# Gathered-expert work planned by stage instead of at one even spacing, in a two-block transformer kernel

## What is computed

```python
# first block: window attention + spatial gating + pooling, gated and merged;
#              memory attention; dense MLP (1024 -> 4096 -> 1024)
# second block: MLA attention (8 heads) and forgetting attention (8 heads), o @ w_o, and then
h2 = _modulate(x, norm2_g, shift2, scale2)
x = x + gate2 * _peer(h2, w_pq, sub_keys, peer_u, peer_v)

def _peer(h, w_pq, sub_keys, peer_u, peer_v):
    qp = (h @ w_pq)...                      # 8 heads x 2 halves of 128
    s1, i1 = lax.top_k(sc[..., 0, :], 16); s2, i2 = lax.top_k(sc[..., 1, :], 16)
    top_s, top_c = lax.top_k(all 16 x 16 sums, 16)
    expert = e1 * 128 + e2; gate = softmax(top_s)       # 16 experts a head, of 16384
    a = h . peer_u[expert]                  # one dot product of 1024 for each expert
    y = sum(gate * gelu(a) * peer_v[expert])
```

## Time and profile before

| | |
|---|---|
| median of 3 runs | 2723.76 us |
| the profiled execution | 2719.11 us, its span 2717.3 us |
| busy in the span | PE 2066.2 us, DVE 1366.1, POOL 1158.2, ACT 457.1 |
| first half's dense part | 0 to 918 us |
| second half's dense part, with the first half's experts | 918 to 1972.8 us |
| the second half's experts alone | 1972.8 to 2717.3 us |

### The profile page before, as it was taken

One profiled execution on the slowest core, in us unless ns is written; L12 is line 12 of the kernel. 1 busy time (PEld: TensorE's weight loads), 2 busy tenths in 40 slices (PEclk: granted clock), 3 DMA queues, 4 the chain that ended last, 5 costly groups with the idle time before them and its releaser, 6 DMA issues.

```text
span 2717.3 us, 27166 instructions
## 1 busy us (share of the span) xinstructions
PE 2066.2 (76%) x9658; PEld 1441.0 (53%) x9658; DVE 1366.1 (50%) x3057; ACT 457.1 (17%) x1123; POOL 1158.2 (43%) x1090
## 2 busy tenths in 40 slices
PE   7899989999989979997999998888923332323334
PEld 5788778887466767875777773454800000000001
DVE  1302136302424986557654466753657575766641
ACT  2311131001442222112210012332100000000000
POOL 2000002000001456544545553454477777777775
PEclk9899989998969989997899988889965556655557
DMA  6244329642415979997999998789799999999998
GB/s 226 69 152 149 132 90 376 214 155 85 136 34 175 390 301 359 394 396 269 341 392 386 381 346 313 281 307 340 264 335 382 352 368 354 379 359 364 367 407 349
DMA packets 214728, 779.19 MB, mean 287 GB/s; under 512 B 23891, under 2 KB 26515, under 8 KB 213571
## 3 DMA queue, kind: packets, MB, share of 16 engines
q0 software_dynamic: 155136, 564.97, 55.0%
q1 hardware_dynamic: 57272, 207.44, 21.5%
q10 hardware_dynamic: 2187, 5.05, 0.5%
HBM read 770.78 MB, written 6.58 MB: 286 GB/s over the span
## 4 chain that ended last, share of the span: by engine, by line
PE 59%; POOL 18%; issue 9%; DVE 8%; DMA 4%; ACT 2%; ACTq 0%; DVEq 0%; POOLq 0%
PE bank L563 43%; POOL main L499 18%; PE bank L732 5%; DMA main<-in_peer_v,idx_v 3%; PE bank L631 3%; PE bank L668 2%; PE bank L686 2%; DVE main L1479 1%; DMA main<-in_peer_u,idx 1%; PE bank L677 1%; PE bank L640 1%; PE bank L980 1%; ACT main L1012 1%; PE bank L694 0%; DVE main L1401 0%
## 5 line engine op out<-in xcount | busy, mean ns | idle before, releaser
L563 PE MATMUL bank<-main,ring 128*128 128x256 f32 x4864 | 1076.8, 383 | 10.3 <-DVE main L1636 4.0
L563 PEld LDWEIGHTS bank<-main,ring 128*128 128x128 f32 x4864 | 928.8, 192 | 167.5 <-issue 28.4
L499 POOL DMA_INDIRECT main<-in_peer_v,idx_v x512 | 550.5, 1075 | 458.5 <-PE bank L732 315.7
L732 PE MATMUL bank<-main,w_wide 128*32 128x512 f32 x2048 | 370.3, 860 | 440.3 <-DMA main<-in_peer_v,idx_v 416.1
L499 POOL DMA_INDIRECT main<-in_peer_u,idx x512 | 570.5, 1114 | 311.7 <-issue 148.5
L1479 DVE CUSTOM_DVE_ANT_0 main<-main 128x1024 f32<-128x1024 f32 x256 | 313.8, 1226 | 245.0 <-DMA main<-in_peer_u,idx 241.4
L732 PEld LDWEIGHTS bank<-main,w_wide 128*32 128x32 f32 x2048 | 73.4, 138 | 670.2 <-issue 669.2
L1479 DVE CUSTOM_DVE_ANT_0 main<-main,h_a 128x1024 f32<-128x1024 f32 x256 | 313.8, 1226 | 203.6 <-DMA main<-in_peer_u,idx 198.0
L1012 ACT ACTIVATE main<-bank 128x256 f32<-128x256 f32 (+4 forms) x346 | 145.6, 439 | 775.6 <-PE bank L563 747.9
L563 PE MATMUL bank<-ring,main 128*128 128x512 f32 (+3 forms) x624 | 239.2, 544 | 9.5 <-ACT main L1012 8.8
L492 POOL DMA_DIRECT2D main<-in_w_ada x48 | 25.3, 533 | 451.8 <-DVE main L1656 451.8
(11 more groups left out here) (219 smaller groups left out, 1368.6 us busy)
## 6 DMA issues: line engine op xcount, KB each, us to landing
ring<-in_w_stream SPq DMA_DIRECT2D x370, 512.0 KB, 5.7
main<-in_w_ada POOLq DMA_DIRECT2D x48, 512.0 KB, 7.3
main<-in_peer_u,idx POOLq DMA_INDIRECT x512, 6.6
main<-in_peer_v,idx_v POOLq DMA_INDIRECT x512, 6.5
main<-in_sub_keys SPq DMA_DIRECT2D x2, 1024.0 KB, 9.3
main<-rows_d SPq DMA_DIRECT2D x1, 1536.0 KB, 10.2
main<-in_xT ACTq DMA_DIRECT2D x1, 1024.0 KB, 5.3
main<-in_memT POOLq DMA_DIRECT2D x1, 1024.0 KB, 8.5
```

Of the source, the lines that this page charges most:

```text
L499: gp.indirect_dma_start(rows_buf[:, slot, :], None, table, bass.IndirectOffsetOnAxis(ap=where, axis=0)).then_inc(landed[slot], 16)
L563: ins = pe.matmul(o, lhsT, rhs, **kw)
L732: last = mm(y_bank[half][s * CG:(s + 1) * CG, :], w_wide[:, lo:lo + CG], (v_rows, u_rows)[second][:, slot, half * 512:(half + 1) * 512], s ...
```

## The change

Six edits:

1. `Pace.dot` is no straight line any more. `plan_dots` gives each stage of the second half a spacing: 3.9 in linear stages, 3.0 in the four attentions, 4.4 in sgu, lat, fox_qk, turn and h2, 6.0 in norms. The first 40 dots come at 3.2 instead of 2.6. The remaining 216 are spread by these shares up to 36 before the end of the dense part on the plan's clock. The last dot is due at 1860.8 (before 1791.6), combine 55 at 1882.0 (1812.8), combine 57 at 1897.2 (1828.0).
2. PE turns the lists of indices (`turn_idx`) 4 later on the plan.
3. PE turns the weights (`turn_w`) ahead of the seventh combine of a pair of heads instead of the eighth.
4. DVE forms the weights (`weigh`) after dot 2 of the next pair instead of dot 6.
5. `route` is in five steps instead of six.
6. `finish` of a half's first tile comes two dots sooner and has a due time of its own.

```diff
-    HEAD, BOTH, TAIL, BEHIND = 2.6, 3.6, 1.9, 6.0
+    HEAD, TAIL, BEHIND = 3.2, 1.9, 6.0
+    LINEAR, ATTEND, BUSY, NORM = 3.9, 3.0, 4.4, 6.0
+    SPACE = dict.fromkeys(STAGES, LINEAR) | dict.fromkeys(("band", "mem", "mla", "fox"), ATTEND) | \
+        dict.fromkeys(("sgu", "lat", "fox_qk", "turn", "h2"), BUSY) | dict.fromkeys(("norm1", "norm2", "norm3"), NORM)
...
+    def plan_dots(self):
+
+        m = self.mark
+        spans = [("pq", 53.0)]
+        for s, nxt in zip(STAGES[1:], STAGES[2:]):
+            spans.append((s, 16.0 if s.startswith("norm") else 65.0 if s == "pq" else m[0, nxt] - m[0, s]))
+        first = m[0, "pq"] + 12.0
+        self.dots = [first + self.HEAD * n for n in range(V_LAG)]
+        last = first + sum(us for _, us in spans) - 36.0
...
     def dot(self, n):
         if n >= HALF_ROWS:
             return math.inf
-        first = self.mark[0, "pq"] + 12.0
-        return first + self.HEAD * min(n, V_LAG) + self.BOTH * max(n - V_LAG, 0)
+        if not self.dots:
+            self.plan_dots()
+        return self.dots[n]
...
                         if q == (4 if ends_half else 1) and k + 1 < NT * PAIRS:
-                            yield math.inf if ends_half else pace.batch(b + q) - 1.0
+                            yield math.inf if ends_half else pace.batch(b + q) + EARLY - 1.0
                             turn_idx(k + 1)
-                        if q == PER_PAIR - 1 and k + 1 < NT * PAIRS:
-                            yield pace.batch(b + q) - 1.0
+                        if q == PER_PAIR - 2 and k + 1 < NT * PAIRS:
+                            yield pace.batch(b + q) + 2.0
                             turn_w(k + 1)
...
                 st(ve.tensor_tensor(oh, oh, per_entry(top_i[:, :]), ALU.mult))
-                yield
                 st(ve.reduce_sum(e_f, onehot[:, :].rearrange("p (k i) -> p k i", i=TOPK), axis=AX_X))
...
-                        if j == 6 and k > k0:
+                        if j == 2 and k > k0:
                             weigh(k - 1)
...
-                        if n == n0 + ROWS_PER_TILE + V_LAG + 4:
+                        if n == n0 + ROWS_PER_TILE + V_LAG + 2:
+                            yield pace.batch(CG * (1 + TH * hf) - 1) + 7.0
                             finish(TH * hf)
```

More of the change, by code:

```diff
@@ L153 @@
 class Pace:
-    HEAD, BOTH, TAIL, BEHIND = 2.6, 3.6, 1.9, 6.0
+    HEAD, TAIL, BEHIND = 3.2, 1.9, 6.0
+    LINEAR, ATTEND, BUSY, NORM = 3.9, 3.0, 4.4, 6.0
+    SPACE = dict.fromkeys(STAGES, LINEAR) | dict.fromkeys(("band", "mem", "mla", "fox"), ATTEND) | \
+        dict.fromkeys(("sgu", "lat", "fox_qk", "turn", "h2"), BUSY) | dict.fromkeys(("norm1", "norm2", "norm3"), NORM)
     def __init__(self):
-        self.mark, self.lin = {}, []
+        self.mark, self.lin, self.dots = {}, [], []
     def at(self, hf, stage, part=0.0):
@@ L163, in at @@
         return a + part * (b - a)
+    def plan_dots(self):
[6 more added lines that the diff above has]
+        last = first + sum(us for _, us in spans) - 36.0
+        steps, t = [], first
+        for s, us in spans:
+            lo, hi = max(t, self.dots[-1]), min(t + us, last)
+            if hi > lo:
+                steps.append((lo, hi, (hi - lo) / self.SPACE[s]))
+            t += us
+        total, todo, done = sum(n for _, _, n in steps), HALF_ROWS - V_LAG, 0.0
+        for lo, hi, n in steps:
+            share = n * todo / total
+            while len(self.dots) < HALF_ROWS and len(self.dots) - V_LAG + 1 <= done + share + 1e-6:
+                self.dots.append(lo + (hi - lo) * (len(self.dots) - V_LAG + 1 - done) / share)
+            done += share
     def dot(self, n):
```

## The result

The changed kernel is slower: 2760.6 us as a median against 2722.5 us for the kernel before in the same session, a ratio of 1.0141 with a 95% interval of 1.0113 to 1.0169. The prediction said 2719, range 2694 to 2742. The profiled execution of the changed kernel has a span of 2763.4 us, that of before 2717.3: 46.1 us to find. The medians are 38.1 us apart; the traced execution of the changed kernel happens to be its slowest of four and that of before is 3.3 us under its median, so some 8 of the 46 us are scatter between executions.

What follows compares the result with a forecast made beforehand. PE was taken to set the pace up to 1972.8 us, then gathers at 1.447 us each. 2719.1 - 29.5 (dense part) + 24.7 (tail) = 2714.3 us, 2719 as a median; range 2694 to 2742.

Steps and rivals of the forecast that it cites:

- Denser attentions: From mla to o2, eight more dots, 10.2 us of DVE, about half hidden, plus late u-rows: +7 us.
- rival B: Mla to o2: the ring of buffers throttles the attentions, DVE stands ahead of masks; +22 us, 2741 in all; chance 0.18.
- the relief ahead of h2: Dense part up to h2: PE's waits for DVE at the stages' seams shrink or go, -44.2 us in sum.
- band, branches and norm1: Later dots spare PE waits at band (-12.5) and branches (-2.5); the turn leaves norm1 (-12 us).
- the five terms behind them: Shorter waits or moved combines: norm2 and norm3 -4, entry of mla -6, o2 -2.2, h2 -5 us.
- Combines moved into pq: Stages where PE has no slack: 40 combines counted instead of 36, 4 x 1.92 = +7.7 us.
- paragraph on the clock: At pq: the emptied gap of h2 may hand over PE at the low clock, 3 us on top.
- What is given back: Tail: about 5 second-half gathers out at the dense part's end, not 25; 17 x 1.447 = +24.7 us, bounds 20 and 29.
- The other edits: Later turn_idx, sooner finish, merged route step, and weigh and turn_w in the tail: in slack or covered, 0 us.
- A: Dense part: larger relief, the wait in lat (8.6) goes too and attentions hide their dots (7); 2704 us; chance 0.32.
- C: Stage seams: steps stay in heaps, DVE stays late, half of the 44 us is missing; +20, 2739 us; chance 0.08.
- D: Tail: it fills by itself, so the dense part's gain doesn't reach the end; given no chance.

Runs made afterwards that it cites:

- The late line: Kernel before with one straight line of dots, HEAD 3.2 and BOTH 3.81, last dot due as in the changed kernel, no spacing by stage: 1.0078, 2744.7 us.
- the old end: Changed kernel with ATTEND 4.4 instead of 3.0 and the last dot due where it was before (1791.6 of the plan instead of 1860.8): 1.0091.

## Why the prediction was wrong

Two steps failed, by about the same amount.

**The first failed step** is the one it called "Denser attentions": +7, bounded above by rival B. It measured 27 us by h2 when ATTEND alone was set back (1886.0 for 1913.2). I had reasoned from PE's 25 us of idle time in mla and fox, as if a wait of DVE could be placed in it. But a dot that waits on DVE stops every mask and normalisation behind it, and PE runs dry after that; in mem the two waits are 13.1 us, and in fox one is 13.4. Rival B had this mechanism (ring, DVE at the head of its queue) and the right sign, at 0.18, but it is only part of the loss: relieving the ring gave back 8.6 us in mla and 1.7 in fox, while taking work off DVE gave 14.3 in fox, mostly as a higher clock. B was priced at +22 for mla to o2 alone, took the clock for constant, and looked at no other attention. The traces show mem losing as well, and the granted clock of fox going from 0.80 to 0.65.

**The second failed step** is the relief ahead of h2, -44.2 in the sum. The late line holds it alone: at the linear stage behind norm1 PE is ahead by 22.7 us (22.1 in the changed kernel), and at h2 by 22.5. So band, branches and norm1 brought 22 of the 27 predicted, and the five terms behind them (norm2 and norm3, entry of mla, o2, h2: 17.2) brought nothing together. A wait that goes at one seam came back at the next: in the late line PE waits 7.9 at lat, 3.8 ahead of mla and 4.2 at its entry, 5.1 for v-rows at the end of o2 and 6.0 at h2. The stay of lat's wait was predicted; it shrank to 4.9 in the changed kernel.

**Combines moved into pq**, +7.7. Six stand in pq (from 1933.7 to 1994.4): 11.5 us. Beside them the second tile of h2 comes 2.8 us behind the first, and the first 32 weight matmuls take 10.06 us instead of 7.17, since PE was handed over at the low level of the clock (0.50 from 1913.2 to 1918.6, 0.71 over these matmuls, where before it was 1.00): 17.2 of the 18.0 us by which the stretch from h2 to the end of pq grew (84.2 for 66.2). The clock part is what the prediction had in its paragraph on the clock by the rule of "TensorE: Matmul & The Clock Gate", Part 1 of the Trainium skill, as 3 us outside the sum; the trace agrees, with 2.9.

**What is given back**, +24.7: 21.5 in the changed kernel's trace. `gather_u(256)` goes out at 1991.75, 5.6 us ahead of the end, with 5 gathers of the second half out by then, both as predicted. But 20 gathers at the rate of before are 29 us, the upper bound, and not 24.7; the changed kernel's tail ran at 1.443 instead of 1.457 us a gather and so lost 7.6 us less. That the trace comes within 3 us of the forecast is partly luck. In the late line the same 20 gathers came with a tail longer by 31.0, beyond the bound of 29.

**The other edits**, 0: between 0 and +10 by the experiment that held them alone.

Put together against the prediction's -29.5 for the dense part: attentions some +20 more than its +7, pq +10 more, and the relief 22 short, 5 of them by norm1 (band's end came 7.4 us sooner, for 12.5) and 17 behind it. That is 52 of the 54 us missed; the rest I can't place.

**The rivals.** A (2704) was refuted. C had the size of the missing relief, half of the 44 us, but not its place: the heap at norm1 did go, and the waits stood at lat, at mla, o2 and h2 instead. D was right to be given nothing. Of the signs named, "mla and fox over 80 us each" is met by fox (98.7 us from mla's last turn to its own) and not by mla (64.2).

## What to carry to other kernels

An in-order engine that serves two streams should be planned by where it will stand, not by its idle share: a consumer placed ahead of its data's earliest arrival costs everything queued behind it, and the other engine's idle time doesn't pay for it. When work is shifted later to relieve seams, price the stage that receives it and the stage behind the end (here 17 and 21 to 31 us against the 22 won) before counting the seams, and don't sum the seams' waits: behind the first relief, the rest moved to the next seam. Keep the density of a prefetched stream at or under what its ring of buffers returns, in every stage. The same dots moved from the attentions to the linear stages with the same end cost 18 us less (1.0074 for 1.0141), but a linear stage made dense enough stopped PE too (10.7 us with the old end).

## What the runs showed of the hardware

The same program differed by 1.3% between chips (2721 and 2757 us for the kernel before) while the granted clock hardly did, and the rate of the gathers in the tail went with it: 775.5 / 531 = 1.460 us each for the straight late line in the first session, 799.4 / 531 = 1.505 for its twin (the same line with the other edits) in the second. The 24 us between these two tails stand in POOL's idle time: in the second POOL has waits that the first doesn't have at all, and the profile doesn't name what ended them.

```profile
POOL main L499 <- remote: 25.5, 11, 4.1
```

Lowering DVE's load alone raised PE's granted clock from 0.73 to 0.78 in mla and fox and shortened the same 616 matmuls by 11 us, without a matmul being changed; with the load of before, other orders of the same work ran fox at 0.66 and 0.69 (above), where the kernel before has 0.80. And u-rows issued in a burst landed in 12.4 us at the median, in the stretch before it in 6.3.
